# Expert rounds of three blocks of 32 token slots in place of two blocks of 64

## What is computed

```python
g_sel = argmax(softmax(h @ w_group) + b_group)            # 4 groups of 8 experts
e_prob = softmax(e_logits of that group); top 2 of e_prob + e_bias
top_w = top_w / sum(top_w) * g_w
# every token goes to 2 of 32 experts: 512 (token, expert) assignments in a layer
y[token] += top_w * ((silu(x @ w_gate[e]) * (x @ w_up[e])) @ w_down[e])
# w_gate, w_up: 1024 x 512, w_down: 512 x 1024, fp32
```

## Time and profile before

| what | value |
|---|---|
| median of 3 runs | 2294.1 us (2293.15 to 2296.13) |
| the profiled execution, its own time | 2292.24 us |
| its span | 2290.4 us |
| TensorE busy | 2093.4 us (91%) |
| VectorE busy | 829.7 us (36%) |
| ScalarE busy | 335.9 us (15%) |
| DMA, mean over the span | 266 GB/s |
| mean granted TensorE clock | 0.959 of full speed |

### The profile page before, as it was taken

The page is one execution under the profiler, slowest core; times in us unless marked ns, Lnnn a source line. Parts: engine busy times, 40 slices in busy tenths (PEclk is TensorE's granted clock), DMA queues, the critical chain, the costliest instruction groups (busy, mean ns, idle before and its releaser), DMA issues.

```text
span 2290.4 us, 26825 instructions
## 1 busy us (share of the span) xinstructions
PE 2093.4 (91%) x9127; PEld 1110.1 (48%) x9128; DVE 829.7 (36%) x1748; ACT 335.9 (15%) x715; POOL 97.1 (4%) x97
## 2 busy tenths in 40 slices
PE   6889999999899999998889998988797998989894
PEld 3434777745467776644433333333673443333331
DVE  1254333322423334444333333333324333333334
ACT  1134100011420002142111110101101110111011
POOL 0000000000000000000000100100000010001000
PEclk9879999999999999999899999999898999999997
DMA  8465344434844443314699999994655899999992
GB/s 269 138 289 224 133 143 164 166 148 185 363 153 143 159 157 141 147 37 165 268 427 427 427 386 427 378 412 189 255 188 209 331 423 426 396 427 395 427 397 97
DMA packets 61262, 609.07 MB, mean 266 GB/s; under 512 B 17345, under 2 KB 18561, under 8 KB 23569
## 3 DMA queue, kind: packets, MB, share of 16 engines
q1 hardware_dynamic: 44720, 595.02, 64.6%
q0 software_dynamic: 12224, 10.18, 1.4%
q10 hardware_dynamic: 4256, 3.06, 0.5%
HBM read 617.65 MB, written 24.12 MB: 280 GB/s over the span
## 4 chain that ended last, share of the span: by engine, by line
PE 81%; DMA 9%; DVE 5%; ACTq 2%; issue 1%; ACT 1%; DVEq 0%; SPq 0%; POOLq 0%
PE ps L1203 30%; PE ps L812 25%; PE ps L1058 13%; DMA big<-in_w_gate 7%; PE ps L1070 6%; PE ps L826 2%; PE ps L1205 2%; ACTq L1527 2%; DMA f_rows<-big 1%; DVE hT L2361 1%; PE ps L1228 1%; PE ps L1197 1%; DVE big L2350 0%; DMA c_res<-f_rows,big 0%; DMA big<-y_rows 0%
## 5 line engine op out<-in xcount | busy, mean ns | idle before, releaser
L1203 PE MATMUL ps<-big,hT 128*64 128x512 f32 x1920 | 852.7, 603 | 48.9 <-DVE big L2350 46.7
L1205 PE MATMUL ps<-big,hT 128*64 x1920 | 852.4, 603 | 0.0
L1203 PEld LDWEIGHTS ps<-big,hT 128*64 128x64 f32 x1920 | 262.7, 139 | 556.7 <-issue 489.1
L2350 DVE TENSOR_SCALAR big<-big 128x2048 f32 x240 | 293.2, 1225 | 530.7 <-PE ps L1205 387.6
L812 PE MATMUL ps<-big,hT 128*128 128x512 f32 (+4 forms) x792 | 299.4, 536 | 15.2 <-DVE hT L1935 10.6
L1058 PE MATMUL ps<-hT,big 128*128 128x256 f32 x1408 | 311.1, 379 | 0.0
L1058 PEld LDWEIGHTS ps<-hT,big 128*128 128x128 f32 x1408 | 267.2, 190 | 52.4 <-issue 18.2
L1205 PEld LDWEIGHTS ps<-big,hT 128*64 128x64 f32 x1920 | 262.6, 139 | 0.2
L812 PEld LDWEIGHTS ps<-big,hT 128*128 128x128 f32 x792 | 143.4, 193 | 160.6 <-issue 140.6
L812 PE MATMUL ps<-big 64*30 64x256 f32 (+14 forms) x704 | 149.4, 488 | 31.7 <-DVE big L2310 7.3
L1070 PE MATMUL ps<-big 128*128 128x512 f32 x352 | 158.4, 593 | 0.4 <-DVE big L2139 0.4
(11 more groups left out here) (319 smaller groups left out, 1161.4 us busy)
## 6 DMA issues: line engine op xcount, KB each, us to landing
big<-in_w_down SPq DMA_DIRECT2D x64, 2048.0 KB, 17.0
big<-in_w_gate SPq DMA_DIRECT2D x64, 2048.0 KB, 19.4
big<-in_w_up SPq DMA_DIRECT2D x64, 2048.0 KB, 19.9
big<-in_dense SPq DMA_DIRECT2D x45, 2048.0 KB, 8.8
big<-in_dense SPq DMA_DIRECT2D x52, 1536.0 KB, 6.7
big<-in_dense SPq DMA_DIRECT2D x5, 1024.0 KB, 7.7
big<-y_rows SPq DMA_DIRECT2D x4, 1024.0 KB, 5.9
f_rows<-big ACTq DMA_DIRECT2D x4, 512.0 KB, 11.0
```

What stands on the lines that cost most here:

```text
L1203: nc.tensor.matmul(ps[SLOTS:P, bank, :], xT[:, k, SLOTS:P], side[:, half, row - half * CH // 2:row - half * CH // 2 + BW], start=start, st ...
L1205: return nc.tensor.matmul(ps[0:SLOTS, bank, :], xT[:, k, 0:SLOTS], experts3[:, bass.ds(here, 1), kind * CH + row:kind * CH + row + BW] .re ...
L2350: ts(side[:, half, :], experts3[:, bass.ds(there, 1), lo:lo + CH // 2].rearrange("p a n -> p (a n)"), 1.0, None, mult).then_inc(s["side_co ...
```

## The change

Blocks have 32 slots instead of 64, and a round takes three consecutive blocks, on column groups 0 to 31, 32 to 63 and 64 to 95; `NB` becomes 48 and there are 16 rounds. The second and the third block's weights are both copied aside, in quarters of a kind: the second's by VectorE, the third's by ScalarE, each with two buffers in turn. All counting is in quarters. TensorE waits for both copies before each quarter. SyncE's order of loads becomes gate of e, down of e-1, up of e. The router's arithmetic is adapted (division by 3 through a multiplication by 171 and a shift). ScalarE's part is written out for all 16 rounds instead of in a loop.

```diff
-SLOTS = 64
+SLOTS, WIDE = 32, 3
+ROWS = SLOTS * WIDE
...
-        side = area(3 * CH, 2, CH // 2)
+        side = area(3 * CH, 2, 2, QW)
...
-                def again(e, q):
-                    halves = sp.value_load(need_i[0:1, bass.ds(e - BPE, 1)], min_val=2, max_val=6 * NPAIR)
-                    for kind in range(3):
-                        sp.wait_ge(done.sem, halves + (done.base + 2 * kind))
+                def again(e, q, kinds):
+                    quarters = sp.value_load(need_i[0:1, bass.ds(e - BPE, 1)], min_val=4, max_val=12 * ROUNDS)
+                    for kind in kinds:
+                        sp.wait_ge(done.sem, quarters + (done.base + 4 * kind))
                         put(kind, e, q)
+
+                def staggered(e, q):
+                    again(e, q, (0,))
+                    again(e - 1, (q + BPE - 1) % BPE, (2,))
+                    again(e, q, (1,))
...
                     row = k * n + c0
-                    nc.tensor.matmul(ps[SLOTS:P, bank, :], xT[:, k, SLOTS:P],
-                                     side[:, half, row - half * CH // 2:row - half * CH // 2 + BW], start=start, stop=stop)
+                    at = row - quarter * QW
+                    for g in (2, 1):
+                        nc.tensor.matmul(ps[g * SLOTS:(g + 1) * SLOTS, bank, :], xT[:, k, g * SLOTS:(g + 1) * SLOTS],
+                                         side[:, g - 1, quarter % 2, at:at + BW], start=start, stop=stop)
                     return nc.tensor.matmul(ps[0:SLOTS, bank, :], xT[:, k, 0:SLOTS],
...
-                        for half in range(2):
-                            pe.wait_ge(copied.sem, copied.at(b * 6 + (2 * kind + half + 1)))
-                            for k in range(4 * half, 4 * half + 4):
+                        for quarter in range(4):
+                            both_copied(b, 4 * kind + quarter)
+                            for k in range(2 * quarter, 2 * quarter + 2):
...
+                def copy(b, there, j):
+                    kind, quarter = j // 4, j % 4
+                    if quarter == 0:
+                        act.wait_ge(s["kind_landed"].sem, s["kind_landed"].at(3 * b + kind + 1))
+                    if b or j >= 2:
+                        act.wait_ge(done.sem, done.at(b * 12 + j - 1))
+                    lo = kind * CH + quarter * QW
+                    nc.scalar.copy(side[:, 1, quarter % 2, :], experts3[:, bass.ds(there, 1), lo:lo + QW]
+                                   .rearrange("p a n -> p (a n)")).then_inc(s["side2_copied"].sem, 1)
...
+                for b in range(ROUNDS):
+                    for j in range(2, 6):
+                        copy(b, there, j)
                     silu(b)
+                    for j in range(6, 10):
+                        copy(b, there, j)
+                    if b + 1 < ROUNDS:
+                        rows_T(b + 1)
+                    for j in range(10, 12):
+                        copy(b, there, j)
+                    if b + 1 < ROUNDS:
+                        there = third(b + 1)
+                        copy(b + 1, there, 0)
+                        copy(b + 1, there, 1)
                     rows_out_(b)
...
                     if quarter == 0:
                         landed(kind, loads)
+                        v.sem_inc(s["kind_landed"].sem, 1)
```

More of the change, by code:

```diff
@@ L768, in load_experts @@
                 after(sp, "route" + tag)
[L769 to L773, removed]
+                again(BPE, 0, (0, 1))
+                whole = (E - BPE - 1) // BPE
+                with sp.Fori(0, whole) as i:
+                    for u in range(BPE):
+                        staggered(i * BPE + (BPE + 1 + u), (1 + u) % BPE)
+                for e in range(BPE + 1 + whole * BPE, E):
+                    staggered(e, e % BPE)
+                again(E - 1, (E - 1) % BPE, (2,))
             def fetch(tag, T):
@@ L1207, in product, with both_copied, turn @@
                                             .rearrange("p a n -> p (a n)"), start=start, stop=stop)
-                def pair(b, first=False, more=True):
-                    here = pe.value_load(tab_i[0:1, 0, bass.ds(b * 2, 1)], min_val=0, max_val=BPE - 1)
+                def both_copied(b, j):
+                    for e in copied:
+                        pe.wait_ge(e.sem, e.at(b * 12 + (j + 1)))
+                def turn(b, first=False, more=True):
+                    here = pe.value_load(tab_i[0:1, 0, bass.ds(b * WIDE, 1)], min_val=0, max_val=BPE - 1)
                     pe.wait_ge(s["xT_done"].sem, s["xT_done"].at(b * 2 + 2))
@@ L1241, in experts @@
                 rows_T(0, 1, first=True)
[L1242 to L1245, removed]
+                turn(0, first=True)
+                with pe.Fori(1, ROUNDS - 1) as b:
+                    turn(b)
+                turn(ROUNDS - 1, more=False)
             lhs = lambda k, c: hT[:, k, c * P:(c + 1) * P]
@@ new lines, in experts @@
+                there = third(0)
+                rows_T(0)
+                copy(0, there, 0)
+                copy(0, there, 1)
+                for b in range(ROUNDS):
+                    for j in range(2, 6):
+                        copy(b, there, j)
+                    silu(b)
+                    for j in range(6, 10):
[8 more added lines that the diff above has]
+                        copy(b + 1, there, 1)
@@ L2340, in landed, with copy @@
                     v.wait_ge(slot_full[BPE * 2 + kind], loads[2] + (16 + 16 * (E // BPE) * layer))
-                def copy(b, there, loads, kind, half, first):
-                    if half == 0:
+                def copy(b, there, loads, j, first):
+                    kind, quarter = j // 4, j % 4
+                    if quarter == 0:
                         landed(kind, loads)
-                    j = 2 * kind + half
+                        v.sem_inc(s["kind_landed"].sem, 1)
                     if j >= 2 or not first:
[L2348 to L2351, removed]
@@ L2353, in pair @@
-                def pair(b, first=False):
-                    there = v.value_load(tab_i[0:1, 0, bass.ds(b * 2 + 1, 1)], min_val=0, max_val=BPE - 1)
-                    loads = [v.value_load(tab_i[0:1, 1 + q, bass.ds(b * 2 + 1, 1)], min_val=0, max_val=16 * E)
+                        v.wait_ge(done.sem, done.at(b * 12 + (j - 1)))
+                    lo = kind * CH + quarter * QW
+                    ts(side[:, 0, quarter % 2, :], experts3[:, bass.ds(there, 1), lo:lo + QW].rearrange("p a n -> p (a n)"),
+                       1.0, None, mult).then_inc(s["side1_copied"].sem, 1)
@@ L2356, in pair, with turn @@
+                def turn(b, first=False):
+                    there = v.value_load(tab_i[0:1, 0, bass.ds(b * WIDE + 1, 1)], min_val=0, max_val=BPE - 1)
+                    loads = [v.value_load(tab_i[0:1, 1 + q, bass.ds(b * WIDE + 2, 1)], min_val=0, max_val=16 * E)
                              for q in range(BPE)]
-                    for j in range(5):
-                        copy(b, there, loads, j // 2, j % 2, first)
+                    for j in range(9):
+                        copy(b, there, loads, j, first)
@@ L2368, in pair @@
                             .then_inc(s["hT_done"].sem, 1)
-                pair(0, True)
-                with v.Fori(1, NPAIR) as b:
-                    pair(b)
+                    for j in range(10, 12):
+                        copy(b, there, loads, j, first)
+                turn(0, True)
+                with v.Fori(1, ROUNDS) as b:
+                    turn(b)
             def combine(name, T, x):
@@ L2689, in experts @@
                 gather(1)
-                for b in range(NPAIR):
-                    if b + 2 < NPAIR:
+                for b in range(ROUNDS):
+                    if b + 2 < ROUNDS:
                         gather(b + 2)
```

134 lines of the change are left out of this document (67 added, 67 removed).

## The result

The changed kernel takes 2345.8 us (median of 4 runs, 2341.7 to 2346.9) against 2293.6 us for the kernel before beside it: a ratio of 1.022, 95% interval 1.0204 to 1.0240. The prediction was slower, 2331 us, between 2290 and 2385. The profiled execution took 2341.71 us, 49.5 more than that of before.

The account below looks back on a forecast made before the run. TensorE and DMA were both taken to run near their limits; with three experts a round, late loads outweigh saved passes: stages +36.8, router +1, +38 on 2292.2 gives 2330, median 1.9 higher, about 2331 us, range 2290 to 2385.

Parts of the forecast that it names:

- Third group free: TensorE's passes: a third column group adds nothing at 0.43 us a pass; 16 rounds instead of 20 save 92 us a stage.
- The rounds against the ring: Expert stages: three experts' gates fill three places, so loads come late; TensorE waits 129 and 122 us, stages sum to +36.8.
- The late loads: Named gate, up and down loads in the expert stages land 1.3 to 5.5 us late: 44 and 31 us in all.
- The dense queue: Rival on expert loads: full rounds' loads come within 15.45 us, nothing is late, 2249 us; chance 0.10.
- that of the third group: Rival on TensorE's passes: the third group is not free, 0.54 us a pass gives +106 us; chance 0.15.
- The low ends taken together: Rival: lone load 7.6 us, first copy 1.0, hidden rows 0.4 quicker, no clock loss: 2285 to 2315 us; chance 0.13.
- The sum: Both expert stages: 518.1 + 505.1 - 492.8 - 493.6 = +36.8 us.
- The schedule: Expert-stage rounds worked out by three rules for load issue and landing, kind start and clock: 518 and 505 us after.
- after a wait of over 6 us: TensorE's clock in the expert stages: passes then take 0.86 us until the clock is back, costing some 2.2 us.
- sensitivity for 3.4 us: Expert stages: if clock loss came already at waits of 3.4 us, the change would cost +48 us.
- Copies hidden: Quarter copies on VectorE and ScalarE fit behind 1.72 us quarters; ScalarE is busy 15 of 23 us a round.
- The router: Three more chained VectorE operations of 0.2 us in each layer, 1 us together.

Follow-up runs that it names:

- e5: The kernel before with the loads of experts 3 to 31 cut to 64 of 4096 columns: 2230.5 us, one run.
- e7: The changed kernel with loads of experts 3 to 31 cut to 64 of 4096 columns and VectorE's register reads spread over the round before: 2052.6 us, one run.
- e2: The changed kernel with the old order of loads (gate, up, down of one expert, then the next): 2391.8 us, one run.
- e1: The changed kernel with each 2 MB load split in two of 1 MB, the first issued when half its place is free: 2313.0 us, ratio 1.008.
- e11: The changed kernel with each 2 MB load split in two of 1 MB, both issued only when the whole place is free: 2346.6 us, ratio 1.0227.
- e3: The changed kernel with VectorE's four register reads for the next round taken between copies of the round before: 2336.2 us, ratio 1.0179.
- e9: The kernel before with the new load order and 2 MB loads halved, the first issued when half its place is free: 2291.2 us, ratio 0.9989.

## Why the prediction was right, and what it had too small

*Third group free:* right, 0.43 us a pass, and TensorE's gain of 92 us a stage real (e5 to e7).

*The rounds against the ring:* right in place and nearly in size. The late loads were those named, the long wait stood before round 4 (15.2 us, forecast 17), and in the second stage before round 9. Moving only the order (e2) or the issue (e1, e11) moved the time as this mechanism asks, e1 by 33 of the 53 us expected. The dense queue, the rival that ends faster, fell: 18.8 us where it needed 15.45. So did that of the third group. The low ends taken together did not come: no load took under 8.0 us, where 7.6 was needed, ScalarE's copy 1.05 and not 1.0, and the low clock cost 57 us and not nothing.

*The sum:* the stages were forecast at +36.8 and came to +47.5 (1031.7 against 984.2). The schedule had the old ones 2.2 us too long and the new ones 8.5 too short. A stage is 16 rounds of 22.93 us, the waits, and the slow passes. Waits: forecast 129 and 122, measured 521.6 - 366.9 - 26.9 = 127.8 and 510.1 - 366.9 - 29.7 = 113.5, together 10 less. Slow passes: forecast 22 and 16 (what is left of 518.1 and 505.1), measured 26.9 and 29.7, 19 more. **The term that was mis-sized is the clock**, and within it the rule "after a wait of over 6 us". The timeline of the changed kernel shows what shorter waits do:

```profile
1504.27 0.62 PE L1218 MATMUL ps<-big,hT 128*32 128x512 f32 x2 [2.52 <-ACT big L1697]
...
1504.70 0.62 PE L1218 MATMUL ps<-big,hT 128*32 128x512 f32 x2
...
1571.76 1.07 PE L1218 MATMUL ps<-big,hT 128*32 128x512 f32 x2 [3.38 <-ACT big L1697]
...
1572.59 1.10 PE L1218 MATMUL ps<-big,hT 128*32 128x512 f32 x2
...
2019.11 0.60 PE L1247 MATMUL ps<-c_ident,hT 96*128 96x96 f32 x2 [2.39 <-DVE hT L2403]
...
2020.59 1.07 PE L1218 MATMUL ps<-big,hT 128*32 128x512 f32 x2
```

After 2.52 us of idleness a pass takes 0.43, after 3.38 it takes 0.83: the granted clock is 1.00 from 1504.3 to 1506 us and 0.50 from 1571.9 to 1574, 2.4 and 1.2 GHz. But no single length of wait parts the two. In the changed kernel none of the 24 waits of 1.3 to 1.6 us was followed by slow passes and each of the 28 waits from 2.79 us up was; between, 2.52 was not and 2.39 was, and in e3 one of 3.18 was not. The trace of before has idle times of TensorE of at most 1.3 us or at least 7.05, so a point between was a guess. The prediction's own sensitivity for 3.4 us, +48, is close to what came, in part by luck: it has neither the slow passes after shorter waits nor the register reads. Those lie in the measured waits, and e3 prices them at 9.6 us; without them the waits would have been some 20 us under the forecast, not 10. So the stages came near the forecast with three errors that partly cancel. The same change of the rule accounts for part of e1: with it the schedule, worked again after the run, gives 496 and 493 for its stages, without it 489 and 486, measured 503.8 and 496.1.

*Copies hidden:* right for the copies (ScalarE's 1045 ns, VectorE's 693), wrong for VectorE's queue, whose four register reads I had not counted. e3 prices them: 9.6 us. That only the first block's weights can be addressed by a register, the reason given for copying at all, no run here tests.

*The router and what lies outside the stages:* +1 forecast, 1.2 between the stages.

The profiled execution is thus 11.7 us over the sum. Of the other 3 us to the median, 2.2 are that this kernel's median stands 4.1 above its profiled run, where I had taken 1.9; the rest is rounding (the terms of the prediction add up to 2331.9).

**Open:** the last 10 us between e1's stages and the schedule (1000 against 989). A rate of 421 GB/s put into the schedule would cover them, but would also have made e11 about 10 us slower than the changed kernel, which it was not. And e9's loss of 6.6 us is shown as a time, with a lower rate beside it, but not traced to single loads. That the clock's part can be had back was only read from passes, not tried with a TensorE kept busy. e2 and e5 to e7 are single runs; their differences of 45 to 178 us are far over the 10.6 us by which repeated runs of one kernel differ at most.

## What to carry to other kernels

When an engine's work shrinks, draw the loop that refills its buffers: landing, copy, use, free, issue, landing. If a round needs as many experts' weights as there are places, that loop (18.8 us here) and not the queue's rate (15.45) sets the pace, and cutting the work moves nothing but waits. Test the parts of a combined change alone; here, with the loads in, the order of loads was the only part that paid (a ratio of 0.994 to 0.996 alone). And where steps get shorter, count what stands between them on the queue, register reads too: four at 0.72 us fit where each of two buffers holds 3.43 us of work, and don't where it holds 1.72.

## What the runs showed of the hardware

- Three 32-column fp32 matmuls run side by side at the rate of one: 0.43 us for three 512-column passes, with weight loads of 115 ns each.
- TensorE falls to 1.2 GHz after idle times of 3.4 us (the passes that follow take 0.83 to 0.86 us), while 2.5 us leave it at 2.4 GHz. After waits of 3.4 to 6 us some four or five passes were slow, after 12 to 15 us four to six: many short waits cost more than one long one.
- A read of a register from SBUF takes VectorE's queue 0.72 us, 0.30 of it the load. The Trainium skill ("DMA: Bandwidth & Descriptors", section "Latency and other measured facts") has a floor of about 600 ns for `tensor_load`; these are 297 to 324 ns, and lower.
- Transfers of 1 MB instead of 2 MB lower a full queue from 427 to 420 to 422 GB/s.
